# One core, two transformer blocks: the first projection stage cut at other blocks, and its modulations summed in five groups by VectorE

## The reference, cut to what matters

```
cs = silu(c)                                      # c: one row of 2048
mod = cs @ w_ada + b_ada                          # w_ada: 2048 x 12288
sh1, sc1, gt1, sh2, sc2, gt2 = split(mod, 6)
h = rmsnorm(x, g_pre_mix) * (1 + sc1) + sh1       # x: 256 rows of 2048
proj = h @ w_in                                   # qa ka va qb kb vb qi ki wi ga gb
```

## Time and profile before

| | before |
|---|---|
| median of three runs | 2583.02 us |
| the profiled execution, its own time | 2583.49 us |
| its span in the profile | 2581.7 us |
| PE busy | 2545.9 us, 99% |
| DVE busy | 1732.7 us, 67% |
| ACT busy | 1208.7 us, 47% |

### The profile page before, as it was taken

One profiled execution on the slowest core, in us unless ns is written; L12 is line 12 of the kernel. 1 busy time (PEld: TensorE's weight loads), 2 busy tenths in 40 slices (PEclk: granted clock), 3 DMA queues, 4 the chain that ended last, 5 costly groups with the idle time before them and its releaser, 6 DMA issues.

```text
span 2581.7 us, 30579 instructions
## 1 busy us (share of the span) xinstructions
PE 2545.9 (99%) x12374; PEld 2113.2 (82%) x12374; DVE 1732.7 (67%) x2308; ACT 1208.7 (47%) x1743; POOL 6.4 (0%) x16
## 2 busy tenths in 40 slices
PE   7999999999999999999999999999999999999998
PEld 4887788887877888888888888878788888888887
DVE  6887988788886866556556565546665575664665
ACT  4534445443446434435444465455564344443443
POOL 0000000000000000000000000000000000000000
PEclk9999999999999999999999999999999999999999
DMA  9994367488885785555555545534545555555553
GB/s 365 384 354 166 120 245 276 182 342 312 336 335 217 264 303 191 199 189 185 203 182 188 206 169 180 195 114 147 196 173 200 182 189 202 179 196 196 179 198 145
DMA packets 80764, 567.11 MB, mean 220 GB/s; under 512 B 9024, under 2 KB 9152, under 8 KB 16112
## 3 DMA queue, kind: packets, MB, share of 16 engines
q1 hardware_dynamic: 79488, 558.09, 58.8%
q0 software_dynamic: 1136, 7.07, 0.7%
HBM read 563.02 MB, written 2.10 MB: 219 GB/s over the span
## 4 chain that ended last, share of the span: by engine, by line
PE 84%; DVE 9%; DMA 3%; ACT 2%; issue 1%; SPq 0%; DVEq 0%; ACTq 0%
PE ps L1074 19%; PE ps L1077 19%; PE ps L1075 19%; PE ps L1118 15%; PE ps L1123 8%; DVE wl L1806 3%; DVE ACC L1827 3%; DMA raw<-stream_in 2%; ACT wh L1422 1%; DVE M L2147 1%; DMA X<-x_in 1%; PE ps L1362 1%; PE ps L1338 0%; PE ps L1197 0%; PE ps L1139 0%
## 5 line engine op out<-in xcount | busy, mean ns | idle before, releaser
L1806 DVE TENSOR_TENSOR wl<-raw,wh 128x1024 fp32r<-128x1024 f32 x845 | 996.8, 1220 | 565.5 <-ACT wh L1422 564.4
L1422 ACT ACTIVATE wh<-raw 128x1024 fp32r<-128x1024 f32 x845 | 847.2, 1049 | 716.9 <-PE ps L1077 578.9
L1077 PE MATMUL ps<-wl,U 128*128 128x512 f32 x1376 | 536.7, 390 | 1.5 <-DVE wl L1806 1.5
L1074 PE MATMUL ps<-wh,U 128*128 128x512 f32 x1376 | 538.2, 391 | 0.0
L1075 PE MATMUL ps<-wh,U 128*128 128x512 f32 x1376 | 535.6, 389 | 0.0
L1118 PE MATMUL ps<-HT,wh 128*128 128x512 f32 x1792 | 449.6, 393 | 0.0
L1074 PE MATMUL ps<-wh,HT 128*128 128x512 f32 x1096 | 437.9, 400 | 6.0 <-DVE M L2147 2.7
L1077 PE MATMUL ps<-wl,HT 128*128 128x512 f32 x1096 | 429.4, 392 | 1.5 <-DVE wl L1806 1.4
L1075 PE MATMUL ps<-wh,HT 128*128 128x512 f32 x1096 | 427.6, 390 | 0.0
L1118 PEld LDWEIGHTS ps<-HT,wh 128*128 128x128 f32 x1792 | 322.8, 189 | 58.6 <-DVE M L2184 0.2
L1077 PEld LDWEIGHTS ps<-wl,U 128*128 128x128 f32 x1376 | 258.3, 188 | 59.8 <-DVE wl L1806 5.8
(11 more groups left out here) (275 smaller groups left out, 1379.3 us busy)
## 6 DMA issues: line engine op xcount, KB each, us to landing
raw<-stream_in SPq DMA_DIRECT2D x497, 1024.0 KB, 4.8
raw<-stream_in SPq DMA_DIRECT2D x16, 896.0 KB, 7.1
raw<-stream_in SPq DMA_DIRECT2D x17, 640.0 KB, 7.3
raw<-stream_in SPq DMA_DIRECT2D x13, 512.0 KB, 4.8
M<-rows_in POOLq DMA_DIRECT2D x6, 1024.0 KB, 6.3
y_out<-X SPq DMA_DIRECT2D x3, 512.0 KB, 2.6
X<-x_in SPq DMA_DIRECT2D x1, 1024.0 KB, 5.2
X<-x_in SPq DMA_DIRECT2D x2, 512.0 KB, 13.8
```

The lines of the kernel that those rows point to most:

```text
L1074: e.matmul(o, ah, H[:, c:c + bw], start=k == k0, stop=False)
L1077: ins = e.matmul(o, ah, L[:, c:c + bw], start=False, stop=end)
L1422: e.activation(H, raw[place[n][0]][:, c:c + w], ACT.Copy).then_inc(*hi.tick(p))
L1806: e.tensor_tensor(L, raw[place[n][0]][:, c:c + w], H.bitcast(F32), ALU.subtract).then_inc(*lo.tick(p))
```

## The change

The cuts differ by slab now. qi goes 0 to 2 and then 2 to 16, qB and kB 0 to 2, 10 and 16, vB and kA 0 to 4, 8 and 16, vA 0 to 8 and 16. The six slabs thus have 16 parts in place of 18. The modulations come in five groups of 2, 2, 4, 4 and 4 blocks. In all of them DVE sums; only the shift of the first group is still PE's, now with the weights as the stationary operand and the silu column as a single moving column. Groups 1 and 2 have two accumulators, `ACC` for even row blocks and `ACC2` for odd ones; an event brings four row blocks (groups 0 and 1) or two (groups 2 to 4), always 1 MB. The first chunk of qi isn't split: its matmuls take the raw fp32 weights and an fp32 `HF`.

```diff
-PHASES = (0, 4, 9, 16)
+GROUPS = (0, 2, 4, 8, 12, 16)
+BORDERS = {"qi": (0, 2, 16), "qB": (0, 2, 10, 16), "kB": (0, 2, 10, 16), "vB": (0, 4, 8, 16), "kA": (0, 4, 8, 16),
+           "vA": (0, 8, 16)}
...
+def group_ks(g, i):
+
+    per = 4 if g < 2 else 2
+    return range(per * i, per * i + per)
...
-    columns = [("s", q, k) for q in (1, 2) for k in range(16)]
-    chunks = phase(0)
-    out += [("p", 0, i) for i in range(4)] + [chunks.pop(0), ("p", 1, 0), ("p", 1, 1), chunks.pop(0), ("p", 1, 2), ("p", 1, 3)]
-    beside(chunks, columns, (1, 2, 2, 2, 2, 2, 2, 2, 1))
-    beside(phase(1), columns, [1] * 16 + [0] * 3)
+    out += group_events(0) + chunks("qi@0") + chunks("qB@0") + chunks("kB@0") + chunks("vB@0", 0, 1) + group_events(1)
+    beside(chunks("vB@0", 1) + chunks("kA@0") + chunks("vA@0", 0, 2), group_events(2), (1, 2, 2, 2, 1))
+    beside(chunks("vA@0", 2) + chunks("kA@1") + chunks("vB@1") + chunks("kB@1", 0, 1), group_events(3), (1, 1, 1, 1, 1, 2, 1))
+    beside(chunks("kB@1", 1) + chunks("qB@1") + chunks("qi@2"), group_events(4), (0, 1, 1, 1, 1, 1, 1, 1, 1, 0, 0, 0, 0, 0))
...
+    for n in (5, 6):
+        split(n + 1)
+        for t in range(2):
+            for b in range(2):
+                add("bank", events[n][1], parts[n], t, b, True, True)
+                evac(events[n][1], t, b)
+        at["done"] = parts[n][-1]
+    for n in range(8, 12):
+        add("ada", n)
+    for j in range(2):
+        split_piece(12, j, only=("ACT",))
+    for t in range(2):
+        for b in range(2):
+            add("bank", "vB@0", parts[7], t, b, True, False)
+            if (t, b) == (1, 0):
+                colsum(11)
+                add("xhalves", 1)
...
+    run("vB@0", begin=1, within=lambda: add("xturn", 2))
+    run("kA@0")
+    run("vA@0", end=2, within=third_pair, hold=True)
+    run("vA@0", begin=2)
+    for name in ("kA@1", "vB@1", "kB@1", "qB@1", "qi@2"):
+        run(name)
+    drain()
...
+            for p in ps if name == "qi@0" else ():
+                n, k, c = pieces[p]["n"], pieces[p]["ks"][0], pieces[p]["c"] + 512 * b
+                e.wait_ge(*(floated_v if k else floated)(("hf", k, t)))
+                e.wait_ge(*arrived(n))
+                ins = e.matmul(o, HF[:, k, 128 * t:128 * t + 128], raw[place[n][0]][:, c:c + 512], start=k == 0, stop=k == 1)
...
+        def shift_sums(n):
+            e.wait_ge(*silu("c"))
+            e.wait_ge(*arrived(n))
+            for i, k in enumerate(group_ks(0, events[n][2])):
+                for j in range(2):
+                    c = 512 * i + 128 * j
+                    ins = e.matmul(bank[4 + 3 * j][:, 0:1], raw[place[n][0]][:, c:c + 128], VT[:, V_C + k:V_C + k + 1],
+                                   start=k == 0, stop=k == 15)
...
+                    if k < len(both):
...
+                        e.tensor_scalar(a, r, cs, None, ALU.mult).then_inc(*acc.tick(*keys))
+                    else:
+                        e.wait_ge(*acc(("sum", g, k - len(both))))
+                        e.scalar_tensor_tensor(a, r, cs, a, ALU.mult, ALU.add).then_inc(*acc.tick(*keys))
```

More of the change, by code:

```diff
@@ L142, in blocks_of @@
     if kind == "s":
[L143 to L146, removed]
+        k0, k1 = GROUPS[name:name + 2]
+        return [("w_ada", k, D * part + 128 * k0, 128 * (k1 - k0)) for k in group_ks(name, i) for part in range(2)]
     w, c0, width, _, _ = SLABS[name]
@@ L367, in run @@
             hooks = {(0, nb - 1): lambda: steps((pace + 1) // 2)}
-            if within:
-                hooks[1, 0] = within
+            if within and i == (end or total) - 1:
+                hooks[0, 1] = within
             many = 1
@@ L441, in run @@
                 colsum(m)
-            pending.extend(sums)
+            if not hold:
+                pending.extend(sums)
             if hooks is head:
@@ L588, in ffn, with sums @@
                 later("rot")
[L590 to L594, removed]
+    def sums(n):
+        add("ada", n)
+        add("shiftsum", n)
     add("xsquare", 0)
     add("xnorm", 0)
-    for n in range(3):
+    sums(0)
+    add("xq", 0, 0)
+    add("xturn", 0, 0)
+    for n in (1, 2, 3):
         sums(n)
-    for p in range(2):
-        add("xq", p, 0)
+    add("xq", 1, 0)
     add("xsquare", 1)
-    sums(3)
     add("xsquare", 2)
-    add("rowcopy", 3)
+    colsum(3)
+    add("constants", 4)
+    native(4)
+    add("xfloat", 0)
     add("xnorm", 1)
     add("xq", 0, 1)
[L608 to L613, removed]
-    add("xq", 1, 1)
[L615 to L622, removed]
+    for b in range(2):
+        add("bank", "qi@0", parts[4], 0, b, True, True)
+        evac("qi@0", 0, b)
+        if b == 0:
+            add("xturn", 0, 1)
+            add("xfloat", 1)
+    add("xsplit")
+    split(5)
+    add("xq", 1, 1)
     for b in range(2):
@@ L959, in turn_keys @@
         if kind == "turnx":
[L960 removed]
+            return [("h", 0, k + i, t) for i in range(2) for t in range(2)]
         if kind == "gm":
@@ L1125, in tile @@
             free[i % 4] = [(evac_v, (name, i))]
-        def row_vec(n):
-            i = events[n][2]
-            if i == 0:
-                for s, k in free[4]:
-                    e.wait_ge(*s(k))
+        def shift_sums(n):
             e.wait_ge(*silu("c"))
             e.wait_ge(*arrived(n))
-            for t in range(4):
-                k = 4 * i + t
-                w = 512 if both_by_pe(n) else 256
-                ins = e.matmul(bank[4][0:1, 0:w], VT[:, V_C + k:V_C + k + 1], raw[place[n][0]][:, 512 * t:512 * t + w],
-                               start=k == 0, stop=k == 15)
-            ins.then_inc(*rowvec.tick(n))
-            free[4] = [(copied, ("row", n))]
@@ new lines, in column_sums @@
+        def column_sums(n, pair):
+            e.wait_ge(ones_set, 1)
+            kind, g, _ = events[n]
+            if kind == "s":
+                o, nt = bank[4 if g == 0 else 7 - 3 * pair], GROUPS[g + 1] - GROUPS[g]
+                for s, k in free[7 - 3 * pair]:
+                    e.wait_ge(*s(k))
+                if g == 0:
+                    e.wait_ge(*mods(("shift", 0)))
+                e.wait_ge(*acc((n, 0)))
+                e.wait_ge(*acc((n, 1)))
+                tiles = (0, 1) if g == 0 else [i * nt + 2 * pair + j for i in range(2) for j in range(2)]
+                for i, j in enumerate(tiles):
+                    both = sums_of(n)
+                    for q, a in enumerate(both):
+                        ins = e.matmul(o[:, i:i + 1], a[:, 128 * j:128 * j + 128], ONES[:, 0:1], start=q == 0,
+                                       stop=q == len(both) - 1)
+                ins.then_inc(*colsum.tick((n, pair), *([(n, "end")] if 2 * pair + 2 == nt else [])))
+                free[4 if g == 0 else 7 - 3 * pair] = [(mods, ("av", 1, GROUPS[g] + 2 * pair))]
+                return
+            if not by_rows(n):
```

337 lines of the change are left out of this document (171 added, 166 removed).

## The result

The changed kernel takes 2592.14 us (median of eight runs, 2591.16 to 2593.24), the kernel before 2582.78 us beside it (eight runs, 2581.17 to 2590.64). The ratio is 1.003, with a 95% interval of 1.002 to 1.0041: slower by 0.3%. The forecast was 2585.0 with a range up to 2590.5, so the time lies outside the range, and the likeliest case ("the same") did not come. The profiled execution took 2591.86 us, 8.4 more than that of before.

What follows compares the result with a forecast made beforehand. PE, busy for 99%, was taken as the bound, with DVE and DMA close. Terms: -8.3 (PE's work) + 4.4 + 2.2 + 3.3 (waits) = +1.6 us on 2583.49, so 2585; range 2576 to 2590.5.

Steps and rivals of the forecast that it cites:

- the likeliest case ("the same"): Whole kernel: time within 0.2% (5.2 us) of the kernel before, chance 0.49.
- the rest of 7.5: First stage before `kiwi`: 7.5 us unexplained by PE's work, part low clock, part small waits, carried over unchanged.
- the signs that I had named as wrong: First stage: column sums without a PE wait, a start later than 23 us, or clock 0.50 outside the start.
- The shift sums of group 0 lie in the wait for the landings; I cost them at nothing.: Start of PE: these sums hide behind loads and add nothing, so projections start at 22.25 us.
- the half-clock price: Start of PE: without cover, shift sums take 3.2 us per group of eight, moving the start by about 2 us.
- Column matmuls until 53.2: First hole, group 1 on PE: sums ready at 51.6 us, eight column matmuls take 1.6 us.
- the clock falls in the holes: Rival, column matmuls of groups 1 and 2: half clock adds up to 4.8 us, 2589.8 us; chance 0.13.
- After that PE and DVE are level ... I add nothing: Groups 3 and 4: DVE needs 86.5 us, PE 91.5, so no wait is added beyond the rest of 7.5.
- the hole at the column sums of group 1: PE near 47 us: waits 4.4 us because group 1's steps on DVE end at 51.6 us.
- The two waits of PE that I had placed in it: Between group 1's column sums and group 2's end: 2.2 us at the next chunk, 3.3 us near 82 us.
- The rival built on it: Steps of groups 1 and 2 on DVE: two accumulators gain nothing, 4.6 us added, 2589.6 us; chance 0.15.
- The first rival (the rest doesn't recur): First stage: with clock 1.00 through the start, up to all 7.5 us vanish, 2577.5 us; chance 0.24.

Runs made afterwards that it cites:

- e7: Changed kernel without 22 of the 32 shift-sum matmuls of group 0 (shift of blocks 0 and 1 incomplete, measures the start alone): 2586.42 us, ratio 1.0013.
- e9: Changed kernel with group 0's shift sums in row form, silu column as stationary operand and 256 columns moving: 2585.85 us, ratio 1.0008.
- e2: Changed kernel with the first two events of group 1 summed ahead of the splits of kB's and vB's first chunks: 2585.86 us, ratio 1.0009.
- e5: Changed kernel with 18 unused multiplications of `ONES` on PE ahead of the column sums of group 1: 2589.74 us, ratio 1.0025.
- e6: Changed kernel with the double event of group 3 moved from the sixth place to the second: 2588.70 us, ratio 1.0023.
- e11: Changed kernel with one accumulator for all groups, so groups 1 and 2 lose their second: 2591.66 us, ratio 1.0026.
- e8: Changed kernel with e2's order for group 1 and e6's early double event in group 3: 2583.57 us, ratio 1.0003.
- e4: Changed kernel with 15 unused multiplications of `ONES` on PE ahead of the first shift sums: 2588.55 us, ratio 1.0019.

## Why the prediction was wrong

In the forecast `kiwi` stood at 215.8 us; measured are 224.86. The 9.1 us are 4.5 (start) + 1.9 (column matmuls of group 1) + 2.6 (behind the end of group 2's sums), with a tenth from rounding, and they lie in three sentences of it. The 2.6 are a net figure. The wait at 132.6 (2.9 us), the two falls of the clock there (half of 3.5 + 3.4) and the longer column matmuls (3.70 for 3.2) make some 6.9 us by my estimate; so some 4 us of the rest of 7.5, which I had carried over from the kernel before, did not come there. That cancelling is luck.

Two of the signs that I had named as wrong were there: a start later than 23 us, and a clock at 0.50 outside the start.

**"The shift sums of group 0 lie in the wait for the landings; I cost them at nothing."** This is the step that failed. They took 3.54 us for the first eight and 10.24 for the other 24, 0.43 each, so 3.4 us for a group that lands in 2.5. The start was 26.77 us, not 22.25. I had worked out the half-clock price (3.2 us a group, "the start would move by about 2 us") and let it stand as an aside without a chance. It was too small as well, for the end of the sums is followed by column matmuls at the same low clock. e7 shows the cause: with few of them the start is 22.29 us and the 4.5 us pass whole to `kiwi`. e9 gives the same start with all of the sums done.

**"Column matmuls until 53.2"** was mis-sized: 3.55 us for the eight, not 1.6, because the clock was at 0.50. The rival "the clock falls in the holes" had this as its first half (2586.6, "within the forecast"), and it came true there. Its second half did not: the 16 of group 2 took 3.70 us at 1.00, and the clock fell only behind them. e2 and e5 show the cause, since the clock stayed at 1.00 in both by different means and both have 1.92 us.

**"After that PE and DVE are level ... I add nothing"** failed at one place. The balance of sums was right, for DVE had enough time in total, but not the order: a double event (5.3 us of steps) and two splits stood ahead of additions that PE needed at 132.6. e6 moved the event, and the gap went from 3.17 to 1.08 us.

What held: the hole at the column sums of group 1 (4.4 forecast, 4.68 measured), its reason (DVE idle for 3.25 us behind ACT, which waits for qB's end), the stretch from there to the end of group 2 (27.1 us forecast; from the low parts' end at 64.3 to 91.5 us are 27.2), and the price of the steps (0.65 and 1.19 forecast, 0.67 and 1.22 measured). That stretch kept its length because DVE bounds it: it was busy for 26.00 of 26 us there. The two waits of PE that I had placed in it, 2.2 us at the next chunk and 3.3 near 82 us, did not show as such. At the next chunk the matmuls at the low clock filled the time, and ahead of the column matmuls of group 2 there were 0.86 and twice 0.17 us for low parts and 0.60 for the sums. The rule of the Trainium skill that I weighed (VectorE: DVE Perf Modes, section The DRAIN you can't avoid) would, as I read it, have made the steps 0.80 us either way. The trace does not agree with that reading: 0.67 with two accumulators and 0.80 with one, for one shape at one place. I had left out a sentence of that section, "A next op that is not held starts earlier", so the difference does not speak against the section as a whole. The rival built on it comes to its result by another way, though: in e11 the second accumulator is worth nothing, because of the columns. The first rival (the rest doesn't recur) failed on its condition, a clock at 1.00 through the start: it was low until 30.6 us, and low three times after that. Of its other half, the small waits, most seem to have gone, as the estimate above says.

Behind `kiwi` I had added 2.7 us for the thirty-sixth block. From `kiwi` to `next` it was 1.5 us (224.0 against 222.5), in the changed kernel and all twelve made from it. The tail that all share happened to be 1.1 us shorter in this execution (2141.1 against 2142.2), which is luck again. So the total was off by 2591.86 - 2585.1 = 6.8 us and `kiwi` by 9.1. What remains open is when the clock falls behind column matmuls and for how long: behind those of group 2 it was low for 3.5 us in the changed kernel, 6.9 in e6 and none in e11, behind those of group 1 it fell in e8 and not in e2, and no run isolates what decides it.

## What to carry to other kernels

Work that is to hide in a wait has to be priced at the clock that TensorE has in that place; here, at the start of the program, that was the low one, and it stayed low under the single-column matmuls. Sum engines against each other for the whole stage, but then walk the queue once more: the three errors here were of order and clock, not of total work. And when a hole is opened, look for what stands ahead of it on the engine that is late (here two events that fitted in the idle time of DVE), before filling it with anything.

## What the runs showed of the hardware

- A matmul with one moving column and a 128x128 fp32 stationary operand took 0.43 to 0.44 us at 1.2 GHz (10.24/24 and 3.55/8) and 0.23 at 2.4 GHz (3.70/16). In a row of them the clock neither rose (the changed kernel, 13.5 to 23.7 us, by the durations) nor stayed up (e4, where it fell at 11.4 us and PE was busy for 10.50 of the next 10.5 us). Under the same sums with 256 moving columns it rose (e9, where it is recorded at 1.00 from 14.9 us). The Trainium skill says that activity releases the throttle (TensorE: Matmul & The Clock Gate, section Part 1: The HAM clock gate); a busy TensorE in the profile was not enough here.
- A dependent accumulation step on VectorE costs more than one that depends on the last but one: 0.80 (e11) against 0.67 us for 512 columns, 1.33 against 1.22 for 1024 (four steps in a row each).
- The same order of work can meet another clock: behind column matmuls of 1.92 us and a wait of 0.3 us it stayed at 1.00 in e2 and was at 0.50 from 53.0 to 56.4 us in e8.
- The code behind the first stage, the same in all the kernels and some 2140 us long, varied by 4 us between executions, more than several of the differences looked for.
